# Final norm of a decoder layer: squares summed by channel tile during the down projection, gain by ScalarE, rows scaled in two halves

## The chip, the cores and the metric

The kernel runs on one core of a Trainium2 chip. The metric is the device time of one execution in microseconds (us); before the change the median of three runs is 2888.81 us (2887.36 to 2890.13).

## What is computed

One step of a decoder with parallel branches, for a prompt of 512 positions and a sample group of 8 rows. Behind attention, pooling and merge come a feed-forward part and the final RMSNorm:

```python
def rms_norm(x, g):
    xf = x.astype(jnp.float32)
    y = xf * lax.rsqrt(jnp.mean(xf * xf, axis=-1, keepdims=True) + EPS)
    return (y * g.astype(jnp.float32)).astype(x.dtype)

z = rms_norm(h, norm_ffn_g)
a = jnp.square(jax.nn.relu(jnp.einsum('btd,df->btf', z, w_up)))
h = h + jnp.einsum('btf,fd->btd', a, w_down)      # d = 2048, f = 8192
y = rms_norm(h, norm_final_g)                     # rows of 2048, fp32
```

The change touches the last line alone: y_prompt is 512 x 2048, y_sample is 8 x 2048.

## The kernel before

The engines run programs written out by hand, and semaphores order them. Inside, the activations lie transposed: channels on the 128 partitions, the 520 positions (two halves of 256 + 4) on the free dimension. `h` has 16 channel tiles of 128 x 520. Every product is done in three parts on values split into a high and a low part (`hi`, `lo`): ScalarE rounds the weights to `hi` (L731), GpSimd subtracts to get `lo` (L1100), and TensorE multiplies (L1811).

The down projection has 8 groups (`group`) of 8 units. A unit c makes the channel tiles 2c and 2c+1 of one group, in the two slots of the PSUM tensor `PP`, 48 matmuls each; VectorE adds each one to `h` (L1763) as soon as it is done, and counts it on `drained`. ScalarE writes `hi` for the unit behind the current one, at the current one's start. `AB`, the other half of PSUM, is free in this stage.

The final norm needs rows, not channels. TensorE transposes `h` with the identity (`y_turn`, L2197): row tile t (four of 128 rows, the fifth has the 8 sample rows) takes 16 transposes, of 128 x 128, into `AB` for even t and into `PP` for odd t. In the last group, the transposes of row tile 0 ride in the units: unit c turns channel tiles 2c-2 and 2c-1 behind its k = 3 (`first_tile`). All else comes behind the last unit: for each row tile ScalarE squares and sums the row straight from PSUM (L1086) and takes the root (L1089), VectorE inverts and refines it (`inverse_root`, L1270 to L1274) and makes the output row by one scalar_tensor_tensor over 2048 columns: PSUM times `rstd` times the broadcast gain `gfin` (L1784). SyncE stores the row tile (L700). TensorE may turn tile t only when tile t-2 has left the same half of PSUM (`s_yn`). `gfin`, the gain on every partition, is loaded at the start of the last group (L696).

## Time and profile before

| | us |
|---|---|
| median of three runs (lowest, highest) | 2888.81 (2887.36, 2890.13) |
| the profiled execution, by its own time | 2887.97 |
| its span, first to last instruction | 2886.2 |
| TensorE busy | 2807.7 (97%) |
| the last unit of the down projection ends | 2859.2 |
| TensorE, VectorE, ScalarE busy from there to 2883.2 | 10.75, 16.46, 11.19 |

The page gives sums over the span. The tail behind the last unit is 1% of it, so the sums say little of it; the chain of waits, the timeline and the table of stretches do. Times in the trace count from the first instruction.

### The profile page before, as it was taken

How to read it: one execution, taken by the hardware profiler on the slowest of the kernel's cores; microseconds unless marked ns; L12 is line 12 of the kernel's file. 1: busy time of each engine (PE TensorE's matmuls, PEld its weight loads, DVE VectorE, ACT ScalarE, POOL GpSimd, SP SyncE). 2: the span in 40 equal slices, each digit the busy share in tenths (PEclk: the TensorE clock that was granted, in tenths of full speed). 3: DMA queues.
4: the chain of work that ended last, by engine and by line, in shares of the span. 5: the costliest groups of instructions: out<-in, count | busy, mean ns of one | idle time of the engine just before them, and what ended most of it. 6: DMA issues, size and time to landing. Idle time of an engine off the chain costs nothing.

```text
span 2886.2 us, 53028 instructions
## 1 busy us (share of the span) xinstructions
PE 2807.7 (97%) x22735; PEld 2748.3 (95%) x22735; DVE 1424.3 (49%) x2194; ACT 861.1 (30%) x1063; POOL 859.5 (30%) x280
## 2 busy tenths in 40 slices
PE   6999999999999999999989999999999999999997
PEld 6988999999999889999979999999989999999997
DVE  4666764664747023321187777777753232322212
ACT  4133222222222133323244434444432222222222
POOL 2433332332336424333300000000034444444431
PEclk9999999999999999999999999999999999999999
DMA  5232332322338434444324343443463233332321
GB/s 190 89 103 89 128 103 71 103 70 78 99 129 295 165 121 133 133 132 129 125 77 140 118 147 123 134 139 118 146 215 118 98 108 127 134 121 88 118 103 60
DMA packets 268734, 354.75 MB, mean 123 GB/s; under 512 B 9706, under 2 KB 199346, under 8 KB 267225
## 3 DMA queue, kind: packets, MB, share of 16 engines
q1 hardware_dynamic: 232067, 296.01, 31.1%
q10 hardware_dynamic: 29262, 30.28, 3.2%
q0 software_dynamic: 7200, 25.30, 2.5%
q8 instruction: 180, 2.95, 0.4%
q14 instruction: 25, 0.20, 0.0%
HBM read 310.55 MB, written 41.19 MB: 122 GB/s over the span
## 4 chain that ended last, share of the span: by engine, by line
PE 84%; issue 6%; DVE 4%; POOL 2%; ACT 1%; DMA 1%; DVEq 1%; ACTq 0%; POOLq 0%; SPq 0%
PE PP L1811 55%; PE PP L2182 18%; PE AB L2182 3%; PE PP L1838 3%; POOL lo L1100 2%; PE AB L1823 1%; PE AB L2015 1%; PE AB L2073 1%; DMA qb<-q_scratch 1%; PE AB L2008 1%; PE AB L1899 0%; DVE prod L1523 0%; ACT AB L752 0%; DVE craw L1730 0%; DVE scS L1458 0%
## 5 line engine op out<-in xcount | busy, mean ns | idle before, releaser
L1100 POOL TENSOR_TENSOR lo<-raw,hi 128x2048 fp32r<-128x2048 f32 x168 | 798.6, 4754 | 1893.3 <-ACT hi L731 1211.6
L731 ACT ACTIVATE hi<-raw 128x2048 fp32r<-128x2048 f32 x168 | 321.4, 1913 | 625.4 <-PE PP L1811 607.1
L1811 PE MATMUL PP<-zh,hi 128*128 128x260 f32 x2080 | 440.7, 293 | 2.0 <-DVE dheld L1312 1.1
L1811 PE MATMUL PP<-fh,hi 128*128 128x260 f32 x2048 | 414.0, 283 | 6.8 <-issue 5.0
L1811 PE MATMUL PP<-zh,lo 128*128 128x260 f32 x2080 | 418.9, 283 | 0.0
L1811 PE MATMUL PP<-zl,hi 128*128 128x260 f32 x2080 | 418.5, 283 | 0.0
L1811 PE MATMUL PP<-fh,lo 128*128 128x260 f32 x2048 | 413.5, 284 | 0.0
L1811 PE MATMUL PP<-fl,hi 128*128 128x260 f32 x2048 | 412.9, 283 | 0.0
L1622 DVE TENSOR_TENSOR lo<-raw,hi 128x1024 fp32r<-128x1024 f32 x224 | 274.3, 1225 | 159.2 <-ACT hi L991 159.2
L1763 DVE TENSOR_TENSOR h<-PP,h 128x520 f32<-128x520 f32 x128 | 89.3, 698 | 500.7 <-PE PP L1811 500.7
L1811 PEld LDWEIGHTS PP<-zh,hi 128*128 128x128 f32 x2080 | 320.3, 189 | 15.2 <-issue 11.6
L1811 PEld LDWEIGHTS PP<-fh,hi 128*128 128x128 f32 x2048 | 316.6, 189 | 7.5 <-issue 6.3
L1811 PEld LDWEIGHTS PP<-zh,lo 128*128 128x128 f32 x2080 | 320.7, 188 | 0.0
L991 ACT ACTIVATE hi<-raw 128x1024 fp32r<-128x1024 f32 x224 | 237.2, 1060 | 279.9 <-DVE raw L1639 75.6
L1811 PEld LDWEIGHTS PP<-zl,hi 128*128 128x128 f32 x2080 | 320.6, 188 | 0.0
L1811 PEld LDWEIGHTS PP<-fh,lo 128*128 128x128 f32 x2048 | 316.6, 189 | 0.0
L1811 PEld LDWEIGHTS PP<-fl,hi 128*128 128x128 f32 x2048 | 315.8, 189 | 0.0
L742 ACT COPY held<-eps 1x1 f32<-1x1 f32 x113 | 21.3, 188 | 368.9 <-PE PP L1811 253.3
L1811 PE MATMUL PP<-mgh,hi 128*128 128x260 f32 x512 | 104.7, 286 | 0.0
L1811 PE MATMUL PP<-mgh,lo 128*128 128x260 f32 x512 | 103.1, 283 | 0.0
L1811 PE MATMUL PP<-mgl,hi 128*128 128x260 f32 x512 | 103.1, 283 | 0.0
L2182 PE MATMUL PP<-a,hi 128*128 128x260 f32 x512 | 96.1, 287 | 5.8 <-DVE stg L1692 5.8
(387 smaller groups left out, 5312.8 us busy)
## 6 DMA issues: line engine op xcount, KB each, us to landing
raw<-in_w_in_dram SPq DMA_DIRECT2D x36, 2048.0 KB, 9.0
raw<-in_w_up_dram SPq DMA_DIRECT2D x32, 2048.0 KB, 9.6
raw<-in_w_down_dram SPq DMA_DIRECT2D x32, 2048.0 KB, 8.0
ffn_scratch<-stg SPq DMA_DIRECT2D x32, 520.0 KB, 2.8
craw<-ffn_scratch SPq DMA_DIRECT2D x16, 1040.0 KB, 6.2
raw<-in_w_out_dram SPq DMA_DIRECT2D x8, 2048.0 KB, 9.6
gates_scratch<-gst ACTq DMA_DIRECT2D x32, 260.0 KB, 3.8
raw<-in_w_attn_out_dram SPq DMA_DIRECT2D x8, 1024.0 KB, 5.4
```

The source lines that it names most:

```text
L731: act.activation(part(hi, kind, u), raw_unit(kind, u), ACT.Copy).then_inc(hi_done, 1)
L991: act.activation(ring_hi[i % 4], up_weights(s, pos), ACT.Copy).then_inc(up_hi, 1)
L1100: pool.tensor_tensor(part(lo, kind, u), raw_unit(kind, u), part(hi, kind, u).bitcast(F32), ALU.subtract)\
L1622: dve.tensor_tensor(ring_lo[i % 4], up_weights(s, pos), ring_hi[i % 4].bitcast(F32), ALU.subtract)\
L1763: dve.tensor_tensor(hm, PP[:, e, :, 0:HC], hm, ALU.add).then_inc(drained[e], 1)
L1811: mm = pe.matmul(PP[:, slot, f, 0:HC], w[:, k, P * e:P * e + P], a[:, f, :], start=(k == 0 and n == 0), stop=(k == nk - 1 and n == 2))
L1823: mm = pe.matmul(out, sta(stas[a], rows), mov(movs[b], rows), start=(n == 0), stop=(n == 2))
L1838: mm = pe.matmul(PP[:, u % 2, 0, 0:QI_N], w[:, k, :], a, start=(k == 0 and n == 0), stop=(k == KD - 1 and n == 2))
L2008: mm = pe.transpose(AB[:, 2, P * t:P * t + P], pr[:, x % 2, P * t:P * t + P], ident[:, :])
L2015: mm = pe.matmul(AB[:, 3, 0:HD], pT[:, x % 2, P * t:P * t + P], vn[:, jj, t, HD * hh:HD * hh + HD], start=(t == 0), stop=(t == i))
L2073: mm = pe.matmul(AB[:, 2 + c, :], pz[:, f, b, :], kv[:, (2 * b + f) % 4, 512 * c:512 * c + 512], start=(b == 0 and f == 0), stop=False)
L2182: mm = pe.matmul(out, w[:, k, :], a, start=(k == 0 and n == 0 and not onto), stop=(k == KH - 1 and n == 2), skip_group_check=onto or opens)
```

## The change

Four things are written differently.

1. The gain. `gfin` (128 x 2048, broadcast) is gone. The gain comes as `gvec`, 16 x 128, at the start of the down projection, TensorE turns it once in unit 0 of the last group, and ScalarE copies it to `gT`: one gain per channel on its partition.
2. The squares. During the last group ScalarE squares each channel tile of `h` as VectorE finishes it (`square_and_gain`) and then multiplies `h` by the gain in place; VectorE adds the squares up in `ssum` (`add_squares`). Behind the last unit five small matmuls, with `ssum` as weights and a column of ones, sum over the partitions and give a column of sums of squares for each row tile. One chain of root, inverse and refinement for all five follows.
3. The rows. A row tile is scaled by `rstd` alone, columns 0 to 1023 by ScalarE, 1024 to 2047 by VectorE, and each half lets TensorE turn half a tile on.
4. TensorE turns the first row tile inside the units behind k = 7, not k = 3, when `h` has its gain (`s_yg`), and turns most of row tile 1 while the squares are added up.

The diff, cut to its core:

```diff
-        sp.wait_ge(pe_halves, 2 * (2 * N_E + (E_GROUPS - 1) * DN_UNITS))
-        sp.dma_start(gfin[:, :], norm_final_g.rearrange("(o d) -> o d", o=1).to_broadcast([P, D])).then_inc(s_gf, 16)
+        sp.dma_start(gvec[:, :], norm_final_g.rearrange("(k p) -> k p", p=P)).then_inc(s_gf, 16)
         for t in range(5):
-            sp.wait_ge(s_yn, t + 1)
+            sp.wait_ge(s_yna, t + 1)
+            sp.wait_ge(s_ynd, t + 1)
...
+        def square_and_gain(m):
+            act.wait_ge(*y_added(m))
+            if m > 1:
+                act.wait_ge(s_ssum, KD + m - 1)
+            act.activation(sq[:, m % 2, :, :], h[:, m, :, :], ACT.Square).then_inc(s_hsq, 1)
+            act.activation(h[:, m, :, :], h[:, m, :, :], ACT.Copy, scale=gT[:, m:m + 1]).then_inc(s_yg, 1)
...
+        for c in range(DN_UNITS):
+            if c < DN_UNITS - 1:
+                split_high(2 * N_E + (E_GROUPS - 1) * DN_UNITS + c + 1, "tall")
+            if c == 0:
+                act.activation(held[0:1, holds % 16:holds % 16 + 1], eps[0:1, :], ACT.Sqrt)
+                act.wait_ge(s_vecT, 2)
+                act.activation(gT[:, :], AB[:, 3, 0:KD], ACT.Copy).then_inc(s_vecd, 1)
+                act.wait_ge(s_vecd, 2)
+            else:
+                for e in range(2):
+                    square_and_gain(2 * c - 2 + e)
...
+        act.wait_ge(s_yss, 2)
+        act.activation(rms[:, 0:5], var[:, 0:5], ACT.Sqrt).then_inc(s_rms, 1)
+        act.wait_ge(s_yrs, 1)
+        for t, n in enumerate(Y_TILES):
+            act.wait_ge(s_yt, 2 * t + 1)
+            dst, src = y_half(t, n, 0)
+            act.activation(dst, src, ACT.Copy, scale=rstd[0:n, t:t + 1]).then_inc(s_yna, 1)
...
+        for m in range(KD):
+            add_output(m)
+            if m > 1:
+                add_squares(m - 2)
+        for m in (KD - 2, KD - 1):
+            add_squares(m)
+        dve.tensor_copy(ssS[:, 0:NB].rearrange("p (f c) -> p f c", f=2), ssum[:, :, HP:HC]).then_inc(s_ssum, 1)
...
+        for t, n in enumerate(Y_TILES):
+            dve.wait_ge(s_yt, 2 * t + 2)
+            dst, src = y_half(t, n, 1)
+            dve.tensor_scalar(dst, src, rstd[0:n, t:t + 1], None, ALU.mult).then_inc(s_ynd, 1)
...
                 def first_tile():
                     for e in range(2):
-                        pe.wait_ge(drained[e], it * (2 * DN_UNITS) + nb)
+                        pe.wait_ge(s_yg, 2 * c - 1 + e)
                         y_turn(0, 2 * c - 2 + e)
...
-                     hooks={3: first_tile} if last and c else None)
+                     hooks={7: first_tile if c else gain} if last else None)
...
+        pe.wait_ge(drained[0], DR_E + E_GROUPS * DN_UNITS)
+        pe.wait_ge(s_yg, KD - 1)
+        y_turn(0, KD - 2)
+        for m in range(KH):
+            mm = y_turn(1, m)
+        pe.wait_ge(drained[1], DR_E + E_GROUPS * DN_UNITS)
+        pe.wait_ge(s_ssum, 2 * KD + 1)
         for t in range(5):
-            if t >= 2:
-                pe.wait_ge(s_yn, t - 1)
+            c = ssum[:, t // 2, P * (t % 2):P * (t % 2) + P] if t < 4 else ssS[:, :]
+            mm = pe.matmul(Y_SUMS[:, t:t + 1], c, ones[:, 0:1], start=True, stop=True)
+        mm.then_inc(s_yss, 1)
+        pe.wait_ge(s_yg, KD)
+        y_turn(0, KD - 1).then_inc(s_yt, 2)
+        for m in range(KH, KH + 4):
+            y_turn(1, m)
+        pe.wait_ge(s_yrs, 1)
+        for m in range(KH + 4, KD):
+            mm = y_turn(1, m)
+        mm.then_inc(s_yt, 2)
+        for t in range(2, 5):
...
+            pe.wait_ge(s_yna, t - 1)
+            turn_half(t, 0)
+            pe.wait_ge(s_ynd, t - 1)
+            turn_half(t, 1)
```

What stands in a row on ScalarE in the last group and behind it, before: the splits of units 2 to 7 follow each other, then come the square and the root of each row tile (`ysq`, `rms`).

```order
L731 ACTIVATE hi<-raw 128x2048 [waits pe_halves,raw_in0] x2
L731 ACTIVATE hi<-raw 128x2048 [waits pe_halves,raw_in1] x2
L731 ACTIVATE hi<-raw 128x2048 [waits pe_halves,raw_in0] x2
L1080 ACT_TABLE_LOAD
L1080 ACTIVATE held<-eps 1x1
L1086 ACTIVATE ysq,ss<-AB 128x2048 [waits y_transposed]
L1089 ACTIVATE rms<-ss,eps 128x1 [waits y_squares_summed]
L1086 ACTIVATE ysq,ss<-PP 128x2048 [waits y_squares_summed,y_transposed]
```

And after, from the first squares on (the part for units 2 and 3 of the group):

```order
L1094 ACTIVATE sq<-h 128x520 [waits drained0]
L1095 ACTIVATE h<-h,gT 128x520
L1094 ACTIVATE sq<-h 128x520 [waits drained1]
L1095 ACTIVATE h<-h,gT 128x520
L747 ACTIVATE hi<-raw 128x2048 [waits pe_halves,raw_in0]
L1094 ACTIVATE sq<-h 128x520 [waits square_sums_added,drained0]
L1095 ACTIVATE h<-h,gT 128x520
L1094 ACTIVATE sq<-h 128x520 [waits square_sums_added,drained1]
L1095 ACTIVATE h<-h,gT 128x520
L747 ACTIVATE hi<-raw 128x2048 [waits pe_halves,raw_in1]
```

Between two splits stand four more instructions of 128 x 520, two that wait for VectorE's additions to `h` and sums, and two that write the gained `h`.

TensorE behind the last unit, before (the first two rows finish row tile 0; 16 transposes make a row tile):

```order
L2197 MATMUL AB<-ident,h 128x128 [waits drained1,drained0]
L2197 MATMUL AB<-ident,h 128x128
L2197 MATMUL PP<-ident,h 128x128 x16
L2197 MATMUL AB<-ident,h 128x128 [waits y_normalized]
L2197 MATMUL AB<-ident,h 128x128 x15
L2197 MATMUL PP<-ident,h 128x128 [waits y_normalized]
L2197 MATMUL PP<-ident,h 128x128 x15
L2197 MATMUL AB<-ident,hS 8x128 [waits sample_columns_copied,y_normalized]
L2197 MATMUL AB<-ident,hS 8x128 x15
```

After:

```order
L2253 MATMUL AB<-ident,h 128x128 [waits y_gained,drained0]
L2253 MATMUL PP<-ident,h 128x128 x8
L2298 MATMUL PP<-ones,ssum 128x1 [waits square_sums_added,drained1]
L2298 MATMUL PP<-ones,ssum 128x1 x3
L2298 MATMUL PP<-ones,ssS 128x1
L2253 MATMUL AB<-ident,h 128x128 [waits y_gained]
L2253 MATMUL PP<-ident,h 128x128 x4
L2253 MATMUL PP<-ident,h 128x128 [waits y_scales_ready]
L2253 MATMUL PP<-ident,h 128x128 x3
L2253 MATMUL AB<-ident,h 128x128 [waits y_first_half_scaled]
L2253 MATMUL AB<-ident,h 128x128 x7
L2253 MATMUL AB<-ident,h 128x128 [waits y_second_half_scaled]
```

The wait for `y_normalized`, one per row tile, has become a wait for each half, and the five products with `ones` stand between the two halves of row tile 1.

VectorE at the end, before (one row tile, and the start of the chain is the same for each of the five):

```order
L1784 SCALAR_TENSOR_TENSOR yrow<-AB,rstd,gfin 128x2048 [waits dve_order]
L1779 TENSOR_SCALAR var<-ss 128x1 [waits y_squares_summed]
L1270 RECIPROCAL rstd<-rms 128x1 [waits root_mean_squares]
L1271 SCALAR_TENSOR_TENSOR var<-rstd,var 128x1 [waits dve_order]
L1273 TENSOR_SCALAR var<-var 128x1 [waits dve_order]
L1274 TENSOR_TENSOR rstd<-rstd,var 128x1 [waits dve_order]
L1784 SCALAR_TENSOR_TENSOR yrow<-PP,rstd,gfin 128x2048 [waits dve_order]
```

After, from the last squares on:

```order
L1811 TENSOR_TENSOR ssum<-ssum,sq 128x520 [waits h_squared,square_sums_added] x2
L1822 COPY ssS<-ssum 128x8 [waits square_sums_added]
L1826 TENSOR_SCALAR var<-PP 128x5 [waits y_squares_summed]
L1828 RECIPROCAL rstd<-rms 128x5 [waits root_mean_squares]
L1829 TENSOR_TENSOR ss<-rstd 128x5 [waits dve_order]
L1830 TENSOR_TENSOR ss<-ss,var 128x5 [waits dve_order]
L1831 TENSOR_SCALAR ss<-ss 128x5 [waits dve_order]
L1832 TENSOR_TENSOR rstd<-rstd,ss 128x5 [waits dve_order]
L1837 TENSOR_SCALAR yrow<-AB,rstd 128x1024 [waits y_transposed,y_scales_ready]
L1840 COPY hS<-h 128x128 [waits y_gained]
L1837 TENSOR_SCALAR yrow<-PP,rstd 128x1024 [waits y_transposed]
```

The small operations stand once, over five columns, ahead of all rows.

## Rows read from the trace of the kernel before

**Rows 1.** The page, part 1: the span and busy time of the engines.
```profile
span 2886.2 us, 53028 instructions
...
PE 2807.7 (97%) x22735; PEld 2748.3 (95%) x22735; DVE 1424.3 (49%) x2194; ACT 861.1 (30%) x1063; POOL 859.5 (30%) x280
```

**Rows 2.** Chain of waits from 2850 us: start, duration, what; both in us.
```profile
2850.54 8.65 PE PP L1811 x72
...
2862.51 0.30 ACT rms L1089
...
2862.84 0.17 DVE rstd L1270
...
2863.68 2.36 DVE yrow L1784
...
2880.89 2.34 DVE ysam L1784
```

**Rows 3.** Timeline of VectorE, last two units: start, duration (us), engine, line, operation.
```profile
2835.71 0.70 DVE L1763 TENSOR_TENSOR h<-PP,h 128x520 f32<-128x520 f32 x1 [5.07 <-PE PP L1811]
2841.70 0.70 DVE L1763 TENSOR_TENSOR h<-PP,h 128x520 f32<-128x520 f32 x1 [5.29 <-PE PP L1811]
2847.47 0.70 DVE L1763 TENSOR_TENSOR h<-PP,h 128x520 f32<-128x520 f32 x1 [5.07 <-PE PP L1811]
```

**Rows 4.** Timeline of ScalarE, last group, same columns; the last bracket is idle time before.
```profile
2835.77 1.92 ACT L731 ACTIVATE hi<-raw 128x2048 fp32r<-128x2048 f32 x1 [9.83 <-PE PP L1811]
2837.71 1.28 ACT L1080 ACT_TABLE_LOAD   x1
```

**Rows 5.** ScalarE by line and shape: count, busy us, mean ns, idle before.
```profile
L731 ACT ACTIVATE hi<-raw 128x2048 fp32r<-128x2048 f32 x168 | 321.4, 1913 | 625.4 <-PE PP L1811 607.1 <-ACT gst L821 13.2 <-issue 2.9
...
L959 ACT ACTIVATE z<-z,vecT 128x520 f32<-128x520 f32 x16 | 11.5, 718 | 0.8 <-DMA residual_scratch<-z 0.8
L978 ACT ACTIVATE sq<-z 128x520 f32<-128x520 f32 x16 | 10.2, 638 | 40.2 <-DVE z L1594 40.2
...
L768 ACT ACTIVATE zh<-AB,vecT 128x520 fp32r<-128x520 f32 x10 | 6.9, 695 | 7.7 <-PE AB L1862 7.6
```

**Rows 6.** VectorE by line and shape, same columns.
```profile
L1598 DVE TENSOR_TENSOR ssum<-ssum,sq 128x520 f32<-128x520 f32 x16 | 11.2, 701 | 11.3 <-ACT sq L978 11.3
...
L1283 DVE TENSOR_SCALAR xt<-xt,rstd 128x2048 f32<-128x2048 f32 x4 | 5.1, 1286 | 0.1
...
L1514 DVE COPY kv<-AB 8x1024 f32<-8x1024 f32 x2 | 2.4, 1213 | 4.8 <-PE AB L2049 4.8
```

**Rows 7.** Timeline of TensorE behind the last unit.
```profile
2860.31 1.91 PE L2197 MATMUL PP<-ident,h 128*128 128x128 f32 x16
2866.08 2.79 PE L2197 MATMUL AB<-ident,h 128*128 128x128 f32 x16 [3.86 <-DVE yrow L1784]
...
2874.48 3.27 PE L2197 MATMUL AB<-ident,hS 128*8 128x128 f32 x16 [2.70 <-DVE yrow L1784]
```

**Rows 8.** Timeline of TensorE near 55 us: eight small fp32 products.
```profile
54.91 1.85 PE L1875 MATMUL AB<-selw,st 120*128 120x8 f32 x16
```

**Rows 9.** Stretches: busy us of each engine (count), PEclk, DMA share, GB/s.
```profile
2866.20:2867.20 1.00, 1.00 (x10) 1.00 (x11) 0.90 (x4) 0.00 (x0) 0.00 (x0) 0.93 0.39 139
2867.20:2868.20 1.00, 1.00 (x6) 1.00 (x5) 1.00 (x1) 0.00 (x0) 0.00 (x0) 0.50 1.02 426
2868.20:2869.20 1.00, 0.67 (x4) 0.27 (x2) 0.98 (x1) 0.29 (x1) 0.00 (x0) 0.50 1.03 410
```

**Rows 10.** Query of tile yrow: the last of the four stores alone.
```profile
DMA to landing us min/median/max: 4.2/4.2/4.2
```

**Rows 11.** Timeline of SyncE's queue: the stores of the output rows.
```profile
2866.05 11.88 SPq L700 DMA_DIRECT2D out_dram<-yrow  x4
2883.25 0.31 SPq L702 DMA_DIRECT2D out_dram<-ysam  x1
```

**Rows 12.** Waits of SyncE's queue, last 3 us: total us, times, longest.
```profile
SPq L704 <- DMA out_dram<-ysam: 2.0, 1, 2.0
```

More of the change, by code:

```diff
@@ L263, in program @@
     eps = small("eps", [P, 1])
-    var = small("var", [P, 2])
+    var = small("var", [P, 8])
     held = small("held", [1, 16])
@@ L1076, in _ @@
                 group(it, g2)
-        for g2 in range(2):
-            group(E_GROUPS // 2 - 1, g2)
-        act.activation(held[0:1, holds % 16:holds % 16 + 1], eps[0:1, :], ACT.Sqrt)
-        for t in range(5):
-            np_ = P if t < 4 else NB
-            act.wait_ge(s_yt, t + 1)
-            if t:
-                act.wait_ge(s_yss, t)
-            act.activation(ysq[0:np_, :], y_banks(t, np_), ACT.Square, accum_out=ss[0:np_, t:t + 1])\
-                .then_inc(s_yss, 1)
-            act.wait_ge(s_yss, t + 1)
-            act.activation(rms[0:np_, t:t + 1], ss[0:np_, t:t + 1], ACT.Sqrt, scale=1.0 / D, bias=eps[0:np_, :])\
-                .then_inc(s_rms, 1)
+        group(E_GROUPS // 2 - 1, 0)
+        for c in range(DN_UNITS):
[10 more added lines that the diff above has]
+        for m in (KD - 2, KD - 1):
+            square_and_gain(m)
+        act.wait_ge(s_yss, 2)
[5 more added lines that the diff above has]
+            act.activation(dst, src, ACT.Copy, scale=rstd[0:n, t:t + 1]).then_inc(s_yna, 1)
         act.wait_ge(s_ko, 16 * (NJ + 1))
@@ L1771, in _ @@
                 group(it, g2)
-        for g2 in range(2):
-            group(E_GROUPS // 2 - 1, g2)
-        dve.tensor_copy(hS[:, :, :].rearrange("p m (f c) -> p m f c", f=2), h[:, :, :, HP:HC]).then_inc(s_hs, 1)
-        for t in range(5):
-            s = slice(0, P) if t < 4 else slice(0, NB)
-            dve.wait_ge(s_yss, t + 1)
-            order.mark(dve.tensor_scalar(var[s, 0:1], ss[s, t:t + 1], 1.0 / D, EPS, ALU.mult, ALU.add))
-            dve.wait_ge(s_rms, 7 + t)
-            inverse_root(s, t)
+        group(E_GROUPS // 2 - 1, 0)
@@ new lines, in add_output, with add_squares @@
+        def add_output(m):
+            dve.wait_ge(pe_halves, 2 * (2 * N_E + (E_GROUPS - 1) * DN_UNITS) + m + 1)
+            dve.tensor_tensor(h[:, m, :, :], PP[:, m % 2, :, 0:HC], h[:, m, :, :], ALU.add).then_inc(drained[m % 2], 1)
+        def add_squares(m):
+            dve.wait_ge(s_hsq, KD + m + 1)
+            dve.tensor_tensor(ssum[:, :, :], ssum[:, :, :], sq[:, m % 2, :, :], ALU.add).then_inc(s_ssum, 1)
+            dve.wait_ge(s_ssum, KD + m + 1)
+        order.mark(dve.memset(ssS[:, :], 1.0))
@@ new lines, in _ @@
+        then(dve.memset(ssum[:, :, :], 0.0))
+        for m in range(KD):
+            add_output(m)
+            if m > 1:
+                add_squares(m - 2)
+        for m in (KD - 2, KD - 1):
+            add_squares(m)
+        dve.tensor_copy(ssS[:, 0:NB].rearrange("p (f c) -> p f c", f=2), ssum[:, :, HP:HC]).then_inc(s_ssum, 1)
+        dve.wait_ge(s_yss, 1)
+        v, q, r = var[:, 0:5], ss[:, 0:5], rstd[:, 0:5]
+        dve.tensor_scalar(v, Y_SUMS, 1.0 / D, EPS, ALU.mult, ALU.add).then_inc(s_yss, 1)
@@ L1782, in _ @@
             if t == 0:
-                dve.wait_ge(s_gf, 16)
-            dve.scalar_tensor_tensor(out=yrow[:, t, :] if t < 4 else ysam[:, :], in0=y_banks(t, s.stop),
-                                     scalar=rstd[s, t:t + 1], in1=gfin[s, :], op0=ALU.mult, op1=ALU.mult).then_inc(s_yn, 1)
+                dve.wait_ge(s_yg, KD)
+                dve.tensor_copy(hS[:, :, :].rearrange("p m (f c) -> p m f c", f=2), h[:, :, :, HP:HC])\
+                    .then_inc(s_hs, 1)
     @block.tensor
```

36 lines of the change are left out of this document (28 added, 8 removed).

## The prediction

> **What bounds the kernel now.** I read the page's first part first: TensorE is busy 2807.7 us of a span of 2886.2, VectorE and ScalarE half of that and less [rows 1]. So what the change does inside the groups of the down projection counts only where TensorE comes to wait for it, and what it does behind the last unit counts in full. Second comes the chain of waits. It stays on TensorE until 2850.54 + 8.65 = 2859.19 us, the end of the last unit (I call it E), and then goes through the final norm: root, small VectorE operations, output row [rows 2]. SyncE issues the first store at 2866.05 and the last, of the sample rows, at 2883.25 [rows 11]. The tail is thus 2886.2 - 2859.2 = 27.0 us in three pieces: 6.9 from E to the first store, 17.2 from there to the last, 3.0 for that one to land and the program to end. Third come the timelines, for the slack in the last group [rows 3, 4], and the prices by shape.
>
> **The last group: does TensorE wait?** A unit lasts 11.76 us (VectorE adds the second tile of the unit before at 2835.71 and 2847.47) and its first half ends at 2841.70 [rows 3]. That half still holds two transposes, 0.2 us, which now come behind it, so TensorE asks for the two gained tiles 5.75 us into the unit. ScalarE starts its split 0.06 us into the unit, and it lasts 1.92 [rows 4]. Behind it now stand two squares at 0.638 and two gains. For a gain the row with the same shape and a scale on each partition is 0.718 (L959) [rows 5]. That makes 0.06 + 1.92 + 2 x (0.638 + 0.718) = 4.69 us, 1.06 before TensorE asks. The second square also waits for VectorE, which adds the output tile (0.70) and the squares (0.70) from the start of the unit [rows 3, 6]: ready at 1.4 us, ScalarE comes to it at 3.3. For GpSimd and the next split nothing changes, since ScalarE has its work done some 7 us before the next unit. VectorE's 16 sums of 0.70 and two memsets lie in idle time of 5 us a tile [rows 3]. The table load of 1.28 us moves from unit 6 [rows 4] to unit 0, where ScalarE has nothing else. The gain's load is 8 KB instead of 1 MB and passes SyncE's queue before it would wait for a low part; I take it at nothing, and even its whole issue (stores take 0.3 us each [rows 11]) stands in front of a wait. One more transpose in unit 0: 0.1 us. So E moves to 2859.3.
>
> **From E to the first store.** Removed: one square (2 us, up to the root at 2862.51 [rows 2]), a root and one chain of small operations for the first tile. Added, in a row behind E:
> - VectorE adds tile 15 (0.70), then the squares of 13, of 14, of 15, each 0.70 [rows 6]. The first may overlap the addition by 0.1, as consecutive additions do not wait for each other. ScalarE squares tile 15 (0.64) behind the sum of 13, and that lies beside the sum of 14. With 0.02 between steps and 0.15 for the copy of the sample columns: 2.95 us.
> - Five products of 128 x 128 weights by one column. Eight fp32 products of such weights by 8 columns take 1.85 us [rows 8], so five take 1.2 at the full clock, to 4.2 us.
> - Scale and add (0.17), root (0.30) [rows 2], and five VectorE operations on five columns at 0.17 to 0.2: 1.45 us, to 5.65.
> - Both halves of row tile 0. ScalarE, 1024 columns from PSUM with a scale: 0.695 for 520 [rows 5] and 504 more at the rate of (1913 - 638)/(2048 - 520) = 0.83 ns: 1.12 us. VectorE, 1024 columns from PSUM: the copy of 1024 from PSUM takes 1.21 [rows 6]. The later one ends at 6.9.
>
> That is 6.9 us against 6.9 now: the head neither gains nor loses. The bounds for VectorE's half are 0.64 (half of the 1.286 for 2048 columns in SBUF [rows 6]) and 1.21; I take 1.21, because that row reads PSUM. The Trainium skill (VectorE: DVE Perf Modes, "Why PSUM operands drop a tier") says that fp32 from PSUM runs at the single rate, which agrees with the pair of rows; by the other rate the head would be 0.55 us shorter.
>
> **From the first store to the end.** The four row tiles go out in stores of 1 MB. Now they come 17.2 us apart from first to last, since for each tile a transposition of 1.9 to 3.3 us [rows 7], a square, a chain and an output row of 2.35 us [rows 2] follow each other. After the change there are three things that may set the pace.
> - TensorE: 8 transposes take 0.27 + 7 x 0.109 = 1.03 us at the full clock (16 in 1.91 at 2860.31) and, by the 16 in 3.27 at the end, some 1.75 at the lower one [rows 7]; directly behind others, 0.87 and 1.52. The rows show both of the two levels, 2.4 and 1.2 GHz: 0.93 after a pause from 2862.2, then 0.50 [rows 9]. Row tile 2 can start at E + 6.8 (ScalarE's first half done). Six halves at the full clock end at E + 12.2, at the lower one at E + 16.15. Then 1.21 for the sample rows' second half, and 3.0 for the last store: E + 16.4 or E + 20.3.
> - ScalarE and VectorE: five halves each of 1.12 and 1.21, 6 us in all. Never the pace.
> - The stores. The first is issued at E + 6.9. Data begin 0.8 us behind the issue (139 of 410 GB/s in the stretch from 2866.20 means a start near 2866.9) and then flow at 426 and 410 GB/s [rows 9]. Four stores of 1.049 MB at 410 GB/s are 10.2 us when one follows the other without a gap. They do, by either clock: at the lower one the third store is issued at E + 6.8 + 1.75 + 1.52 + 1.21 = E + 11.3, and is needed at 12.0 for the flow to go on; the fourth at 14.3, needed at 14.6. The data end at E + 17.9; the sample rows, 64 KB, come 0.2 later. A store of 1 MB issued alone lands after 4.2 us [rows 10], of which 0.8 + 2.6 are start and data, so 0.8 to 1.0 is the receipt; and from the last landing (2.0 us of waiting behind the issue [rows 12], 2885.56) to the end of the span are 0.65 us. Sum: E + 18.1 + 1.0 + 0.65 = E + 19.75.
>
> The stores set the end at E + 19.75, TensorE at E + 20.3 only if TensorE ran at the lower clock throughout. Most pauses behind the change are shorter than the one of 3.86 us of before [rows 7], so I expect a mixture and take the stores: 2859.3 + 19.8 = 2879.1. Against 2886.2 that is 7.1 us less, 0.25%. What was gained is the row loop; the stores become the bound and, against E + 16.4 at the full clock, keep 3.3 us of what the engines alone would give.
>
> The Trainium skill (DMA: Bandwidth & Descriptors, Specifications) gives a limit of about 358 GB/s for one core to HBM. Two whole stretches stand above it here, so the rows decide; by the rule the four stores would take 11.7 us, the end would be 2880.6, and the gain 5.6.
>
> **Own time and median.** The profiled execution took 2887.97 us, 1.8 more than its span. With the same 1.8 the changed kernel takes 2880.9. The median of the runs before is 0.84 above the profiled one; I give the time on the median's level: 2888.8 - 7.1 = 2881.7 us. The runs before lie 2.8 us apart, and less than 0.2% (5.8 us) cannot be told from no change.
>
> **The rivals.**
> - *The tail runs at the lower clock, or the stores are slower in a row than one by one.* For it: after each pause of TensorE the row shows 0.50 for 3 us [rows 9], and behind E it is busy with 10 transposes, pauses for 1.9 us, does 1.2 us of small products and pauses again. The five products then take 2.2 instead of 1.2, which moves all that follows by 1.0, and TensorE sets the end: 2859.3 + 1.0 + 20.3 = 2880.6. No row of before shows four stores in a row either; a rate lower by a seventh would give the same end. Against it: the first transposes behind the pause from 2862.2 to 2866.1 still began at 0.93. Gain 5.0 to 5.8, time 2883.2: faster, but hardly to be told. Chance 0.2. By the Trainium skill's limit (DMA: Bandwidth & Descriptors, Specifications) the stores alone would bring this case about.
> - *More than forecast.* Stores at the better of the two stretches, 426 GB/s [rows 9], save 0.4 us, a receipt of 0.8 saves 0.2, and a VectorE half at its lower bound 0.55: 1.15 us more in all, 2880.5. Chance 0.13.
> - *ScalarE too late in the last group: slower.* Mechanism: TensorE stands in front of `s_yg` at 5.75 us of each of units 1 to 7, with the second half of the unit queued behind it. Price: 7 times the lateness. ScalarE has 1.06 us of slack; the gain of the tail is eaten at a lateness of 7.1/7 = 1.0 us, and slower by 0.2% starts at 1.85, so ScalarE's four new operations would have to take 2.71 + 1.06 + 1.85 = 5.6 instead of 2.7 us. One way there: a table load of 1.28 us [rows 4] between Square and Copy. That gives 2.71 + 4 x 1.28 = 7.8 us, a lateness of 4.1 and 28 us in all: 2881.7 + 28.5 = 2910. Against it: in the order of instructions a table load stands only once in the last group, ahead of the first square, and today the square and the root of a row tile follow each other without one [rows 2]. Chance 0.04.
>
> **How the numbers follow.** Forecast 0.63 (gain 5.9 to 7.9), slower cover 0.2, more 0.13, slower kernel 0.04. Faster by over 0.2% is nearly all of the first (a measured median scatters by 1 us, which takes 0.03 to 0.05 from it), a third of the second, and the third: 0.77. Within 0.2%: 0.19. Slower: 0.04. The range: from 2881.7, up to the case of the lower clock and 1 us of scatter, 2884.6; down to the faster stores and the same scatter, 2879.3.
>
> **What the profile after would show.** Right: transposes in the group without idle time on TensorE and E within 0.2 us of 2859.3; the first store near 2866.2; four stores whose issues lie 7 us from first to last or less, and GB/s near 410 without a gap from 2867 to 2877; the last store landing with the fourth; span near 2879.1. Wrong: idle time of TensorE on ScalarE's `h` in units 1 to 7 (the slower case); a PEclk of 0.5 from 2863 on with the stores issued at the pace of the transposes; stores that flow far from 410 GB/s; or a first store later than 2867, which would mean that sums, products or the chain of five columns cost more than their rows.

## The result and the profile after

The changed kernel takes 2884.75 us (median of 20 runs, 2879.74 to 2889.04), the kernel before in the same comparison 2889.68 us (20 runs, 2885.7 to 2894.7): ratio 0.9983, 95% interval [0.9977, 0.9989]. That is 4.9 us less, where 7.1 were forecast, and the time lies 0.15 us above the range on record. It is 0.17% less, with an interval of 0.11 to 0.23%; the prediction had given a gain of over 0.2% a chance of 0.77. Means over more runs are steadier than medians of one comparison. Over all comparisons the kernel before has a mean of 2889.42 us (157 runs) and the changed one of 2884.40 (43 runs), with standard errors of 0.19 and 0.40: a gain of 5.0 +- 0.45 us.

The page's first part of the changed kernel, which answers to [rows 1]:
```profile
span 2883.6 us, 53107 instructions
...
PE 2812.1 (98%) x22746; PEld 2753.4 (95%) x22746; DVE 1426.6 (49%) x2194; ACT 874.5 (30%) x1087; POOL 857.8 (30%) x280
```
TensorE is busy 4.4 us longer than before although it got only eleven instructions more. So its matmuls ran slower somewhere, and the span's 2.6 us of gain may hide more. To see it, split the span at E, the end of the last unit. The chain of waits of the changed kernel, which answers to [rows 2] (start, duration, what):
```profile
2857.91 5.16 PE PP L1867 x43
...
2863.77 0.70 DVE ssum L1811
...
2864.55 0.65 ACT sq L1094
...
2865.29 0.71 DVE ssum L1811
...
2866.34 1.38 PE PP L2298 x10
...
2867.95 0.22 ACT rms L1116
...
2869.24 1.11 PE PP L2253 x4
...
2870.38 3.67 PE AB L2253 x16
```
E is 2863.06, 3.9 us later than before, and the tail is 2883.6 - 2863.1 = 20.5 us against 27.0. The tail alone gains 6.5 us. The stores, which answer to [rows 11] and [rows 12], from SyncE's timeline and from its waits:
```profile
2870.59 7.05 SPq L704 DMA_DIRECT2D out_dram<-yrow  x4
2879.04 0.30 SPq L706 DMA_DIRECT2D out_dram<-ysam  x1
```
```profile
SPq L708 <- DMA out_dram<-yrow: 3.3, 1, 3.3
...
SPq L708 <- DMA out_dram<-ysam: 0.3, 1, 0.3
```
First store at E + 7.5. Behind the last issue SyncE waits 3.3 us for a row store and then only 0.3 for the small one, so the flow of the big stores sets the end. Stretches of 1 us, which answer to [rows 9] (busy time of each engine, PEclk, DMA share, GB/s):
```profile
2867.20:2868.20 1.00, 1.00 (x7) 1.00 (x7) 0.18 (x2) 0.21 (x1) 0.00 (x0) 0.56 0.06 16
...
2871.20:2872.20 1.00, 1.00 (x7) 1.00 (x6) 0.63 (x1) 0.30 (x1) 0.00 (x0) 0.50 0.90 377
2872.20:2873.20 1.00, 1.00 (x6) 1.00 (x5) 0.00 (x0) 0.81 (x1) 0.00 (x0) 0.50 1.02 410
...
2876.20:2877.20 1.00, 1.00 (x12) 0.80 (x10) 1.00 (x1) 0.38 (x1) 0.00 (x0) 1.00 1.06 442
...
2880.20:2881.20 1.00, 0.00 (x0) 0.00 (x0) 0.00 (x0) 0.00 (x0) 0.00 (x0) 0.89 1.07 434
2881.20:2882.20 1.00, 0.00 (x0) 0.00 (x0) 0.00 (x0) 0.00 (x0) 0.00 (x0) 0.50 0.69 156
```
Data flow without a gap from about 2871.2 to 2881.6, at 377 to 442 GB/s. In the last group ScalarE does what the change gave it. Its timeline in a unit, which answers to [rows 4], with the table load of unit 0 ahead:
```profile
2771.00 1.28 ACT L1105 ACT_TABLE_LOAD   x1
...
2780.97 1.92 ACT L747 ACTIVATE hi<-raw 128x2048 fp32r<-128x2048 f32 x1 [5.87 <-PE PP L1867]
2782.80 0.62 ACT L1094 ACTIVATE sq<-h 128x520 f32<-128x520 f32 x1
2783.32 0.71 ACT L1095 ACTIVATE h<-h,gT 128x520 f32<-128x520 f32 x1
2783.94 0.62 ACT L1094 ACTIVATE sq<-h 128x520 f32<-128x520 f32 x1
2784.47 0.72 ACT L1095 ACTIVATE h<-h,gT 128x520 f32<-128x520 f32 x1
```
ScalarE is through 4.3 us into the unit, and TensorE shows no wait there.

Where do the 3.9 us ahead of E come from? The down projection itself (first product to E) takes 744.9 us against 744.6. The rest, 3.6 us, lies upstream in code that the change leaves as it was. Two pairs of stretches show the pattern. Of the kernel before:
```profile
934.00:937.00 3.00, 0.10 (x1) 0.10 (x2) 2.85 (x2) 0.00 (x0) 2.49 (x1) 1.00 0.24 90
937.00:940.00 3.00, 3.00 (x26) 3.00 (x27) 2.74 (x5) 0.48 (x2) 0.00 (x0) 1.00 0.79 242
```
and of the changed one:
```profile
934.00:937.00 3.00, 0.55 (x3) 0.55 (x4) 2.62 (x3) 0.00 (x0) 2.04 (x1) 0.73 0.15 60
937.00:940.00 3.00, 3.00 (x16) 3.00 (x16) 2.80 (x6) 0.00 (x0) 0.00 (x0) 0.50 0.95 290
```
Behind the same pause TensorE is granted 2.4 GHz in one execution and 1.2 in the other, and does 26 or 16 matmuls in 3 us. In 3 of the 17 profiled executions below (before, b_third, gvec_late) the clock does not fall at this pause, and in 14 it does. Of the 3.6 us, 2.1 are there at the first product with `ath` (1056.6 us against 1054.5), 3.5 at the first with `mgh` (1249.5 against 1246.0), and no more than 0.1 comes after that.

### The profile page after: what moved, and what is told of

Read it like the earlier page. It is cut to its first block, busy times and chain, and to the rows that moved or that the text cites. A ratio compares the mean times of both kernels' runs of the same rounds, so it can differ in the third digit from the quotient of the medians.

```text
span 2883.6 us, 53107 instructions
## 1 busy us (share of the span) xinstructions
PE 2812.1 (98%) x22746; PEld 2753.4 (95%) x22746; DVE 1426.6 (49%) x2194; ACT 874.5 (30%) x1087; POOL 857.8 (30%) x280
## 3 DMA queue, kind: packets, MB, share of 16 engines
q8 instruction: 180, 2.95, 0.4%
## 4 chain that ended last, share of the span: by engine, by line
PE 83%; issue 6%; DVE 4%; POOL 2%; ACT 1%; DVEq 1%; DMA 1%; ACTq 0%; POOLq 0%
PE PP L1867 54%; PE PP L2238 18%; PE AB L2238 3%; PE PP L1894 3%; POOL lo L1131 2%; PE AB L1879 1%; PE AB L2071 1%; PE AB L2129 1%; DVE prod L1554 1%; PE AB L2064 1%; DMA qb<-q_scratch 1%; PE AB L1955 0%; ACT AB L768 0%; DVE craw L1761 0%; DVE scS L1489 0%
## 5 line engine op out<-in xcount | busy, mean ns | idle before, releaser
L1794 DVE TENSOR_TENSOR h<-PP,h 128x520 f32<-128x520 f32 x112 | 78.2, 699 | 418.7 <-PE PP L1867 418.7
L758 ACT COPY held<-eps 1x1 f32<-1x1 f32 x113 | 21.3, 188 | 371.1 <-PE PP L1867 255.6
```

Source lines behind the costliest of these rows:

```text
L1794: dve.tensor_tensor(hm, PP[:, e, :, 0:HC], hm, ALU.add).then_inc(drained[e], 1)
```

## The experiments

In the table E is the end of the last unit, "down" the time from the first product of the down projection to E, and "tail" the rest of the span, all of one profiled execution; means are over all runs of the kernel, with the standard error. The pooled means are those above. A mean of ten runs has an error of 0.5 to 1.0 us, so what a kernel gains or loses by a microsecond is read from "down" and "tail", not from its mean.

| kernel | mean us (runs) | down | tail | first store |
|---|---|---|---|---|
| before | 2889.42 +- 0.19 (157) | 744.6 | 27.0 | E + 6.9 |
| changed | 2884.40 +- 0.40 (43) | 744.9 | 20.5 | + 7.5 |
| group_only | 2892.3 (11) | 744.9 | 29.3 | + 8.2 |
| squares_x4 | 2901.9 (1) | 764.1 | 20.4 | + 7.4 |
| pe_busy | 2883.3 (9) | 744.8 | 20.4 | + 7.4 |
| rows_dve | 2883.9 (11) | 744.8 | 21.7 | + 8.6 |
| half_bytes | 2883.5 (10) | 744.9 | 19.0 | + 8.4 |
| early_adds | 2882.7 +- 0.5 (11) | 748.2 | 19.9 | + 6.9 |
| short_head | 2882.6 +- 0.9 (11) | 747.9 | 19.6 | + 5.9, + 6.5 |
| gvec_late | 2883.5 +- 0.6 (11) | 744.8 | 21.3 | + 8.3 |
| b_gvec8 | 2894.3 +- 1.0 (12) | 750.5 | 27.1 | + 6.9 |
| short_late | 2881.5 +- 0.6 (10) | 744.8 | 19.0 | + 5.9, + 6.5 |

**Both kernels again, unchanged** (b_again, a_again; later b_third, b_fourth, a_third, for what differs upstream).

> The kernel before, unchanged, profiled once more and timed against itself. Theory (pauses): the start of the down projection (first product with fh, 2114.6 us before, 2118.2 us after the change) differs from run to run by up to 4 us, because the granted clock of TensorE after its pauses near 937, 1070 and 1200 us falls in some runs and not in others; so this profile may show any value of 2112 to 2120 and a ratio of 1.000 with an interval of about 0.0006. Rival (upstream cost of the change): the kernel before starts the down projection at 2114.6 within 0.5 us every time. Second rival (the tail of before is not a fixed 27.0 us): its transposes take 1.9 to 3.7 us a tile as the clock happens to be, so the tail from the last matmul to the end is 24.5 to 28.5 us and here differs from 27.0 by over 0.5.

> The changed kernel, unchanged, profiled once more and timed. Theory (pauses): tail 20.5 us within 0.3, since the stores set it and not the clock; start of the down projection anywhere in 2112 to 2120; median 4.5 to 7 us under before. Rival (upstream cost): start of the down projection at 2118.2 again within 0.5, and 4 us or less under before.

Measured: ratio 1.0 [0.9991, 1.0009] and 0.9984 [0.9975, 0.9993]. The tails repeat, 27.1 and 20.4, but the down projection starts at 2117.3 and 2119.8, where the first pair has 2114.6 and 2118.2. So the start scatters in both kernels, neither has a fixed one, and the 3.6 us between the first pair are not by themselves a cost of the change.

> The kernel before a third time. Tail 27.0 within 0.3 once more if its clock falls cost the same in every run; start of the down projection anywhere in 2112 to 2120.

> The kernel before, one more look. Theory (chance upstream): over the looks at both kernels the start of the down projection scatters by the same 2 us or so, and its means differ by less than 1 us. Rival (upstream cost of the change): the four looks at before lie lower than those at kernels with the change by over 1.5 us in the mean.

> The changed kernel a third time, for the mean. Profiles so far: tail 20.5 and 20.4. Pooled means: before 2889.4 (84 runs), the changed kernel 2884.4 (31 runs), 1.3 more than before less the 6.3 that tail and group give together. Theory (chance: clock falls upstream differ from run to run, spread 2.4 us): the mean of these runs is 2882.5 to 2884. Rival (a cost upstream of some 1.5 us): 2884.5 to 2886.

Measured: starts 2114.9, 2116.7 and 2119.3; ratios 1.0 [0.9992, 1.0009] and, for a_third, 0.9978 [0.9969, 0.9986]. In b_third and a_third the down projection itself took 746.1 and 748.2; that came back in the last experiments below. Whether the change costs something upstream stays open. The mean of a_third, 2884.4 +- 0.95, lies between what its theory and its rival said. The start is 2115.9 +- 0.7 in the mean of the four executions of before, and 2117.5 +- 0.6 in the mean of the nine of kernels with the change up to then (2117.2 with the two that came later, 2119.1 for the changed kernel's own three). The difference of 1.6 +- 0.9 us is just over the 1.5 that b_fourth's rival named, but under two standard errors.

**The work of the last group alone** (group_only): the kernel before, with the gain's small load, the squares, sums and gains of the changed kernel, into tiles that its old tail doesn't read, and with the transposes of the last group behind k = 7.
```diff
+            act.activation(sq[:, m % 2, :, :], h[:, m, :, :], ACT.Square)...
+            act.activation(craw[:, m % 8, :, :], h[:, m, :, :], ACT.Copy, scale=gT[:, m:m + 1])...
...
-                        pe.wait_ge(drained[e], it * (2 * DN_UNITS) + nb)
+                        pe.wait_ge(s_yg, 2 * c - 1 + e)
```


> The additions of the change up to the last matmul, with the tail of before: gain loaded and turned, squares and gains by ScalarE (the gained tiles go to a scratch tile), sums by VectorE, all unused; transposes behind k = 7; the row loop and gfin as before. Theory (what ScalarE and VectorE do in the last group is free, and what stands before it is unchanged): tail 27.0 us, down projection 0.2 to 0.3 us longer than 744.6, time within 0.1% of before: ratio 1.0001. Rival (the 1.6 us by which the medians gain less than the tails come from something that the change costs further up): ratio 1.0006, some 1.8 us slower.

Measured: ratio 1.0011 [1.0002, 1.002], down 744.9, tail 29.3. The group's work costs 0.3 us there. The tail was forecast at 27.0; that it is longer has its reason in VectorE's timeline of this kernel: three sums stand ahead of the old tail.
```profile
2859.99 2.23 DVE L1817 TENSOR_TENSOR ssum<-ssum,sq 128x520 f32<-128x520 f32 x3
2862.26 0.23 DVE L1828 COPY hS<-h 128x128 f32<-128x128 f32 x1
```
The mean lies 2.9 +- 0.7 us above that of before, and tail (2.3) and group (0.3) make 2.6 of it. For a cost further up, with the small load at the changed kernel's place, 0.3 +- 0.7 us are left.

**How much room has ScalarE?** (squares_x4: three more squares of each tile 0 to 13, into the same buffer, each waiting for the one before).
```diff
+            if m < KD - 2:
+                for i in range(3):
+                    act.activation(sq[:, m % 2, :, :], h[:, m, :, :], ACT.Square)...
```


> The changed kernel with each square of tiles 0 to 13 done four times by ScalarE, each waiting for the one before. It measures the price of ScalarE being late in the last group. In the trace after the change ScalarE is done 4.3 us into a unit and TensorE asks at 5.75: slack 1.45. Six more squares a unit at 0.55 to 0.75 us (the waits for itself included) are 3.3 to 4.5 us, so ScalarE is 1.9 to 3.1 us late in each of 7 units. Theory (TensorE waits with the second half of the unit behind it, price 7 times the lateness): last matmul 13 to 22 us later, as idle time of TensorE put down to ScalarE's h. Rival (the lateness is caught up by later units): under 5 us in all.

Measured: 2901.89 us in the one run, down 764.1, that is 19.2 more. TensorE's waits in the last group of this kernel:
```profile
PE AB L2257 <- ACT h L1099: 15.0, 6, 2.5
```
ScalarE now ends 8.3 us into a unit instead of 4.3, and 2.5 of these 4.0 us reach TensorE. The room was thus about 1.5 us (forecast 1.06). The wait comes in six units, not in seven: in the last one ScalarE has no split to do. Each of the six gets 2.7 us longer, and behind two of them the granted clock falls (0.72 from 2818 to 2821 and 0.60 from 2848 to 2851 us), which adds 1.5 us each: 16.2 + 3.0 = 19.2. The slower rival of the prediction had the right mechanism, with six as the factor where it took seven, and was far from its threshold.

**Does TensorE's clock set the tail?** (pe_busy: the transposes ahead of and behind the sums done three times, so that TensorE's pauses shrink, the one ahead of the sums from 2.3 us to 0.6).
```diff
-        for m in range(KH):
-            mm = y_turn(1, m)
+        for _ in range(3):
+            for m in range(KH):
+                mm = y_turn(1, m)
...
-        for m in range(KH, KH + 4):
-            y_turn(1, m)
+        for _ in range(3):
+            for m in range(KH, KH + 4):
+                y_turn(1, m)
```


> The changed kernel with TensorE kept at work in two pauses of the tail: the first 8 transposes of row tile 1 are done three times, and the next 4 three times. Theory (stores set the end): the granted clock stays at 1.00 through the row loop, the transposes of row tiles 2 to 4 take 5.7 us instead of 7.6, the sums come 0.2 us earlier, and the tail is 20.2 to 20.5, as before that. Rival (TensorE's clock sets the tail): 2 us shorter, 18.5.

Measured: ratio 0.9977 [0.9968, 0.9987]; tail 20.4, as without it. TensorE's timeline behind E:
```profile
2869.04 1.97 PE L2253 MATMUL AB<-ident,h 128*128 128x128 f32 x16 [0.49 <-ACT yrow L1121]
2870.84 1.91 PE L2253 MATMUL PP<-ident,h 128*128 128x128 f32 x16
2872.59 1.91 PE L2253 MATMUL AB<-ident,hS 128*8 128x128 f32 x16
```
The sixteen transposes of row tile 2 take 1.97 us instead of 3.67, and the end stays where it was. Behind the first store TensorE doesn't matter.

**VectorE does both halves** (rows_dve).
```diff
-            act.activation(dst, src, ACT.Copy, scale=rstd[0:n, t:t + 1]).then_inc(s_yna, 1)
...
+            dve.tensor_scalar(dst, src, rstd[0:n, t:t + 1], None, ALU.mult).then_inc(s_yna, 1)
```


> The changed kernel with both halves of every row tile scaled by VectorE, one after the other (1.28 us each), and nothing by ScalarE. It takes away the sharing of the rows and leaves the early sums of squares. First store 1.3 us later (E + 8.85). VectorE then needs 2.56 us a row tile, as much as a store needs (2.56 us at 410 GB/s), and the sample rows come at E + 6.15 + 12.9 = 19.0. Theory (stores set the end): tail 20.5 + 1.3 to 1.6 = 21.8 to 22.1, still 5 us under 27.0. Rival (the sharing makes most of the gain): 3 us or more over 20.5.

Measured: ratio 0.9982 [0.9973, 0.9991]; first store 1.1 us later (forecast 1.3), tail 1.1 longer, 21.7, just under the forecast. Ten halves on one engine still stay ahead of the stores: only the later first store is paid.

**Half of the bytes** (half_bytes: columns 1024 to 2047 of the prompt rows are not stored).
```diff
-                sp.dma_start(y_prompt[0, P * t:P * t + P, :], yrow[:, t, :])...
+                sp.dma_start(y_prompt[0, P * t:P * t + P, 0:1024], yrow[:, t, 0:1024])...
```


> The changed kernel storing columns 0 to 1023 of the prompt rows only; the other half of y_prompt is left out. Theory (stores set the end): the flow takes half as long and the last thing to land is the small store of the sample rows, issued at E + 16.0: tail 18.6 to 19.0 instead of 20.5. Rival (the engines set the end and the stores lie beside them): 20.5 within 0.3.

Measured: ratio 0.9977 [0.9968, 0.9987], tail 19.0, which is 1.5 us less than in the changed kernel. In this execution the granted clock fell at the start of the small products, and the first store went out at E + 8.4 instead of + 7.5; by the sum below whole rows would then have ended at + 21.4, so the saving lies between 1.5 and 2.4 us. With half of the bytes the sample rows set the end, and they are issued at E + 16.0 as in the changed kernel: the engines' own pace is close behind the stores'.

**The last sums earlier** (early_adds: on VectorE the squares of tiles 13 and 14 are added ahead of output tile 15).
```diff
-        for m in range(KD):
+        for m in range(KD - 1):
             add_output(m)
...
+        add_squares(KD - 3)
+        add_squares(KD - 2)
+        add_output(KD - 1)
+        add_squares(KD - 1)
```


> The squares of channel tiles 13 and 14 are added before VectorE waits for the last product, so behind it stands one addition of squares, not three. If the tail is head + a flow of stores: the head (last matmul to first store, 7.53 us) gets 0.73 shorter, the store flow stays 10.3 us, the tail is 19.8 instead of 20.5. If TensorE's clock sets the tail: the same 0.7 or anything between -1 and +1, with gaps in the flow of stores.

Measured: ratio 0.9979 [0.997, 0.9988]; first store at E + 6.87, tail 19.85. VectorE's timeline across E shows it: the sums are done while TensorE still multiplies, and one is left.
```profile
2857.42 2.23 DVE L1811 TENSOR_TENSOR ssum<-ssum,sq 128x520 f32<-128x520 f32 x3
2862.76 0.70 DVE L1807 TENSOR_TENSOR h<-PP,h 128x520 f32<-128x520 f32 x1 [3.11 <-PE PP L1869]
2864.16 0.70 DVE L1811 TENSOR_TENSOR ssum<-ssum,sq 128x520 f32<-128x520 f32 x1 [0.70 <-ACT sq L1094]
```

**A shorter head** (short_head: as early_adds, the squares of tile 15 go to TensorE as they are, in products that accumulate, and row tile 0 is scaled in quarters and stored in halves).
```diff
+            if t < 4:
+                c = sq[:, (KD - 1) % 2, t // 2, P * (t % 2):P * (t % 2) + P]
+                pe.matmul(Y_SUMS[:, t:t + 1], c, ones[:, 0:1], start=False, stop=True, ...)
...
+                sp.dma_start(y_prompt[0, 0:P, 0:1024], yrow[:, 0, 0:1024]).then_inc(s_yo[0], 16)
...
+                sp.dma_start(y_prompt[0, 0:P, 1024:D], yrow[:, 0, 1024:D]).then_inc(s_yo[0], 16)
```


> As early_adds, and more: the squares of tile 15 are not added by VectorE but by five more small matmuls onto the sums; TensorE's turn of the rest of row tile 1 waits for the sums to be read, not for the scales; row tile 0 is scaled in four quarters and stored in two halves. By the sum of rows: sums ready at E + 3.2 instead of 4.67, scales at 4.65 instead of 6.13, first store (512 KB) 0.85 later at E + 5.5 instead of 7.53. If the flow of stores sets the end, the tail is 18.5 us (20.5 less 2.0) and the time about 7 + 1.5 to 2 us under before. If TensorE sets the pace once the head is shorter, half of that.

Measured: ratio 0.9978 [0.9969, 0.9987]; tail 19.6, where 18.5 was expected. The half stores go out at E + 5.88 and + 6.54, 1.65 us before that of the changed kernel, and only 0.96 of it arrives at the end. The forecast first half store was E + 5.5. Counted from the second half store, 19.59 - 6.54 = 13.05.

**The sum of the tail.** Where the row tiles are stored whole, the tail is the issue of the first store plus 13.0 us: 20.55 - 7.54 (changed), 20.42 - 7.48 (a_again), 20.68 - 7.69 (a_third), 19.85 - 6.87 (early_adds), 20.39 - 7.43 (pe_busy), 21.65 - 8.62 (rows_dve), 20.36 - 7.42 (squares_x4) and, below, 21.26 - 8.31 (gvec_late) all lie between 12.94 and 13.03. What comes before the first store counts in full, and of what was varied behind it (the pace of TensorE and of VectorE) nothing counts. The two kernels with a first row tile in halves give 13.05 (short_head) and, below, 12.45 (short_late) from the second half; why these two differ isn't known.

The head itself isn't fixed. With the same code in it, the first store goes out at E + 7.4 to + 7.7 in four executions, and at + 8.3 and + 8.4 in two (gvec_late, half_bytes), where the clock fell at the start of the small products. Over these six the head is 0.3 us longer in the mean than the 7.5 of the first profile.

**What is left upstream.** The tail's 6.5 us less 0.3 in the group make 6.2, and the mean gains 5.0 +- 0.45, so 1.2 us are missing, 2.7 standard errors. The clock in the head may make 0.3 of it. Another candidate is the gain's small load. SyncE issues it between its wait for the stores of the feed-forward product and the load for group 1. Where those stores land late, everything behind them is late. SyncE's timeline in a_third, an execution of the changed kernel:
```profile
2108.62 6.92 SPq L679 DMA_DIRECT2D h<-residual_scratch  x4
2115.64 2.62 SPq L640 DMA_DIRECT2D ffn_scratch<-stg  x1
2128.43 0.35 SPq L694 DMA_DIRECT2D gvec<-in_norm_final_g_dram  x1
2128.84 0.96 SPq L663 DMA_DIRECT2D craw<-ffn_scratch  x2
```
and in the profiled execution of the changed kernel:
```profile
2107.51 4.80 SPq L679 DMA_DIRECT2D h<-residual_scratch  x4
2113.94 1.08 SPq L640 DMA_DIRECT2D ffn_scratch<-stg  x1
2125.21 0.35 SPq L694 DMA_DIRECT2D gvec<-in_norm_final_g_dram  x1
2126.65 0.94 SPq L663 DMA_DIRECT2D craw<-ffn_scratch  x2
```
Here SyncE is free early, and stands 1.1 us between the two, in front of the low parts of group 0, which come 8.4 us after the first product; the small load is hidden. In a_third the four loads of the residual took 6.9 us instead of 4.8, the second wait is over already, and the small load's 0.41 us go onto the load for group 1. VectorE stands in front of that load before it adds the next two output tiles to `h`, in a_third and in the changed kernel's profile:
```profile
2135.16 0.70 DVE L1761 SCALAR_TENSOR_TENSOR craw<-craw 128x520 f32<-128x520 f32 x1 [7.43 <-DMA craw<-ffn_scratch]
```
```profile
2131.87 1.06 DVE L1761 SCALAR_TENSOR_TENSOR craw<-craw 128x520 f32<-128x520 f32 x1 [5.24 <-DMA craw<-ffn_scratch]
```
That is 15.9 against 13.7 us after the first product. Of the 2.2 us, only 0.4 are the small load's; 0.7 are the lateness of SyncE ahead of it, and 1.1 the load's own time to land (6.3 us from its issue instead of 5.2). TensorE then waits 2.9 us instead of 1.0, and its clock falls:
```profile
2137.00:2140.00 3.00, 2.65 (x14) 2.68 (x15) 2.72 (x5) 2.36 (x4) 0.77 (x1) 0.63 1.05 388
2140.00:2143.00 3.00, 3.00 (x22) 3.00 (x22) 0.00 (x0) 0.52 (x1) 3.00 (x1) 0.80 0.50 182
```
It was so in 3 of the 10 profiled executions with the small load at this place up to then (a_third, early_adds, short_head; down 748), and, without the fall of the clock, in 1 of 4 of before (b_third: load at + 8.9 us, down 746.1). In a fourth of the ten, rows_dve, the second wait was over too, but the load was only 0.2 us late (+ 8.7) and TensorE's wait stayed at 1.0. So late stores happen without the small load as well; whether it adds the fall of the clock can't be told from so few.

The load taken from that place (gvec_late):
```diff
-        sp.dma_start(gvec[:, :], norm_final_g.rearrange("(k p) -> k p", p=P)).then_inc(s_gf, 16)
         down_loads(0, first=True)
+        sp.dma_start(gvec[:, :], norm_final_g.rearrange("(k p) -> k p", p=P)).then_inc(s_gf, 16)
```


> The changed kernel with the load of the gain's column form issued by SyncE behind the load for group 1 of the down projection instead of ahead of it. Theory A (the load in SyncE's queue costs): SyncE reaches the load for group 1 about 0.4 us sooner, TensorE's wait near 2132 is 1.0 us or less, the clock fall behind it becomes rarer, the down projection takes 744.6 to 744.9 us; mean about 2883.2, 1.2 under the changed kernel's 2884.4. Theory B (the missing 1.3 us are chance, where the clock falls): the wait is shorter by 0.4 at most, the mean stays at 2884.4 within 0.8.

Eight such loads put there in the kernel before (b_gvec8):
```diff
+        for i in range(8):
+            sp.dma_start(gvec[:, i, :], norm_final_g.rearrange("(k p) -> k p", p=P)).then_inc(s_yn2, 16)
         down_loads(0, first=True)
```


> The kernel before with eight small loads (never used) that SyncE issues between its wait for the stores of the feed-forward product and the load for group 1. Theory A: eight issues of 0.35 to 0.4 us put the load for group 1 about 3 us later; TensorE's wait near 2132 grows from 1.0 to about 4 us, the clock falls behind it, the down projection takes 748 to 750 us instead of 744.6, and the mean rises from 2889.4 to 2892.5 to 2895. Theory B: the load for group 1 has room ahead of it, and the down projection stays at 744.6 to 745.5 us, the mean within 1 us of before.

And the later load with the shorter head (short_late):

> The half-row start of the tail together with the later load of the gain's column form. By both theories the tail is 19.6 us as in the run with the half-row start. Theory A: down projection 744.6 to 744.9 us, mean about 2882.0. Theory B: mean 2882.6 to 2883.4. It is also the candidate for the fastest version.

Measured for b_gvec8: ratio 1.0016 [1.0006, 1.0026]. SyncE's timeline and TensorE's wait in it:
```profile
2121.42 4.53 SPq L693 DMA_DIRECT2D gvec<-in_norm_final_g_dram  x8
2125.99 0.97 SPq L661 DMA_DIRECT2D craw<-ffn_scratch  x2
```
```profile
PE PP L1816 <- DVE h L1768: 4.9, 1, 4.9
```
The load for group 1 goes out 4.1 us later than before (12.6 after the first product instead of 8.5), the wait grows by 3.9, and the clock fall behind it makes 5.9 us of it in the down projection; the mean rises by 4.8 +- 1.0. So the place has little cover against eight loads, as theory A says.

Measured for gvec_late: ratio 0.9979 [0.997, 0.9988]; mean 0.9 +- 0.7 below the changed kernel, the load for group 1 at + 8.5. The profiled executions of gvec_late and short_late both have early stores (the residual's loads took 4.9 us), so neither shows the case in which the place matters. The profiled tail of gvec_late is 21.3, since here the clock fell already during the small products:
```profile
2862.54 1.69 PE L2298 MATMUL PP<-ones,ssum 128*128 128x1 f32 x8 [2.32 <-DVE ssS L1822]
```
For short_late: ratio 0.9972 [0.9963, 0.9982]; mean 1.1 +- 1.1 below short_head; tail 19.0, where both theories had 19.6. The two together give 0.95 +- 0.6 us for the load's place, 1.6 standard errors, and part of short_late's may be its shorter tail. The direction is that of theory A, and the case with eight loads shows the mechanism, but an effect of the single load isn't shown and its size isn't settled: in proportion to b_gvec8 it would be 4.8 x 0.4/4.1 = 0.5 us. Group_only, with the load at the same place, leaves 0.3 +- 0.7 for all costs upstream. So the 1.2 us stay open; with 0.3 for the head and 0.5 for the load, the 0.4 left is within the error of the means.

short_late is the fastest version of all: 2881.5 us, 2.9 +- 0.7 less than the changed kernel and 7.9 less than before.

## Why the prediction came out wrong

Direction, the bound of the tail and its mechanism were right; the size was too large by 2.2 us. The step that failed is the sum of the head, "the head neither gains nor loses": it came out at 7.5 us where 6.9 stood. Beside it fails the gain's load, which was put at nothing for a reason that doesn't hold in every execution, and 1.2 us of gain are missing whose cause stays open.

- **TensorE in the last group: right.** ScalarE was done at 4.3 us (forecast 4.69), TensorE asked at 5.75 and did not wait; group_only confirms that the work fits, and squares_x4 gives a room of 1.5 us (forecast 1.06) and a price of six times the lateness (forecast seven). E was to move by 0.1; the down projection grew by 0.3.
- **"The head neither gains nor loses": wrong, the largest term that the tail shows.** First store at E + 7.5 instead of 6.9. The sum took the gaps between operations too small. Addition, three sums and copy took 3.15 from E (2.95 in the sum); the products 1.38 with 0.14 of waiting ahead (1.2), since the clock fell within them (in pe_busy and squares_x4, where it didn't, they took 1.25, and in gvec_late and half_bytes, where it fell at their start, 2.1 to 2.2); the halves 1.28 on VectorE (1.21). The chain between was as forecast.
- **"The stores set the end": right.** From first issue to end 13.0 us against 12.85 in the sum. The receipt was 1.35 instead of 1.0, the start about 0.65 instead of 0.8, two misses that partly cancel. The flow of 410 GB/s held; the Trainium skill (DMA: Bandwidth & Descriptors, Specifications) gives about 358 GB/s for a core, and as before whole stretches of stores stand above it, here up to 442. pe_busy shows that TensorE's clock had no part behind the first store.
- **The rival of the lower clock: half of it happened.** PEclk was 0.56 to 0.50 from 2867.2 to about 2874. Behind the first store this cost nothing. Ahead of it the rival was right: where the clock fell at the start of the products, the first store came 0.8 to 0.9 us later (gvec_late, half_bytes), near the 1.0 that the rival gave. Only its second part, TensorE setting the end, did not happen.
- **VectorE from PSUM: right.** 1.28 us for 1024 columns, nearly the price of 2048 from SBUF [rows 6], as the Trainium skill (VectorE: DVE Perf Modes, "Why PSUM operands drop a tier") has it.
- **"The gain's load ... I take it at nothing": the step whose reason failed.** It was said to stand in front of a wait. It does in six of ten executions, in which the stores ahead have landed 6.8 to 7.6 us after the first product. In the other four (8.3 to 9.8 us) that wait is over already, and the 0.4 us push the load for TensorE's next group. What it costs in the mean isn't shown: 0.5 us by proportion, 0.95 +- 0.6 by the means.
- **The level.** The three runs shown, median 2888.8, lie 0.6 below the mean of 157. With a standard deviation of 2.4 us for a single run, a median of three has an error of over 1.5 us; the forecast allowed 1.

In sum: 0.6 for the head, 0.15 for the flow, 0.2 for the group, 0.6 for the level and the 1.2 that neither tail nor group explains make 2.75 of the 2884.75 - 2881.7 = 3.05 us; the rest is, within rounding, that the median of the 20 runs lies 0.35 above the mean of the 43. For the 1.2 us the prediction had no term.

## What to carry to other kernels

When the end is a row of stores that follow each other without a gap, the time to the first store is what counts; sum it with the gaps between dependent operations, and look there, not behind it, for the next gain. A DMA issue "in front of a wait" is free only as long as that wait ends last in every execution: read the times at which a queue is free in several executions before calling it nothing. Where a kernel's runs scatter by 2.4 us, compare a change of 5 by its stages in the profile, and take the times from tens of runs. The stages too need several executions: the tail of the kernel before repeated within 0.1 us in four, but that of the changed kernel's code varied with the clock by 0.9 us, and its down projection from 744.8 to 748.2.
